# A two-layer transformer with 32 experts: the first four experts' tokens are gathered in two parts

## The chip, the cores and the metric

The kernel runs on one core of one Trainium2 chip, in float32 throughout. The metric is the time of one execution on the device, in microseconds (us). A core has a matrix engine (TensorE, PE in the profile), a vector engine (VectorE, DVE), a scalar engine (ScalarE, ACT), a general engine (GpSimd, POOL) and SyncE (SP), which here does nothing but issue loads. The engines run their own instruction streams side by side and wait for each other through semaphores. 16 DMA engines move data from the chip's memory to the core's.

## The reference: what is computed

256 tokens of width 1024 pass through two hybrid layers (latent attention, a short convolution, a spatial gate, block attention), and then through two layers of attention, each followed by a mixture of experts. Only the mixture matters here:

```python
gates = g_prob * e_prob                      # each token: 1 group of 4, 2 experts of its 8
experts = g_idx * EXPERTS_PER_GROUP + e_local
...
xs = x_pad[row_tok].reshape(n_blocks, MOE_BLOCK, D)      # gather the tokens of each expert
def expert_block(args):
    xb, e = args
    return (jax.nn.silu(xb @ w_gate[e]) * (xb @ w_up[e])) @ w_down[e]
ys = lax.map(expert_block, (xs, block_expert)).reshape(n_rows, D)
out = jnp.zeros((N + 1, D), ys.dtype).at[row_tok].add(ys * row_gate[:, None])[:N]
```

There are 32 experts in each of the two layers. An expert has three matrices, gate and up of 1024 by 512 and down of 512 by 1024, 2 MiB each (2.097 MB); so each expert stage reads 96 matrices, 201 MB.

## The kernel before, in words

An expert stage takes its 32 experts in 8 quads (q = 0 to 7) of four experts (j = 0 to 3). Each expert has room for 32 tokens, so a quad has 128 columns.

- **Gather** (`gather(q)` of `experts`, line 946 on TensorE). A product with a 0/1 selection matrix `SEL` (tokens by 128 columns, written by VectorE in `select`) picks the quad's tokens out of the normalised activations `XH` and turns them at once. 8 chunks of the width, 2 tiles of tokens each, make 16 products with a stationary operand of 128x128 and 128 moving columns; in float32 the profile records each as two instructions, hence x32. Chunks 0 to 3 go to bank 0 and ScalarE moves them to `XG` (with scale and bias), chunks 4 to 7 to bank 1, and VectorE moves them. The records of these products are on line 460, the helper `product`.
- **Gate and up** (line 983). For expert j TensorE multiplies its 32 columns of `XG` with the gate matrix (m = 0), then with the up matrix (m = 1): 8 chunks times 4 column groups, 64 records for each matrix. ScalarE applies silu (line 2067), VectorE multiplies (line 1170), TensorE turns the result (`hidden`, line 456).
- **Down** and **combine**: products with the four down matrices (lines 1017, 1030 and 1046), scaling by VectorE, a product that adds the results to the tokens' rows (line 1076).

TensorE runs, in this order: `gather(0)`; experts 0 to 3 of quad 0; down; `gather(1)`; combine; experts 4 to 7; and so on. The gather of a later quad stands ahead of the down products of the quad before it.

**Loads.** SyncE issues all matrices in the order of their use, into 9 slots of 2 MiB (5 of `ring`, 4 in `AR`). The function `plan` fixes at build time which matrix follows which in a slot. Before a load is issued (line 2586), SyncE waits until the last product that reads the slot's matrix before is done; nothing else holds it back. When an expert stage starts, all nine slots are full: gate and up of experts 0 to 3 and the first down matrix. Three matrices are given back early: expert 0's gate in four quarters, its up in two halves and expert 1's gate in two halves (`PARTS`, semaphore `parts`), so their successors are loaded in eight issues on line 2578, six MiB in all. Expert 1's up is the first to be given back whole.

```python
if c < NC - 1 and c % n == n - 1:
    ins.then_inc(sem("parts"), 1)
```

Of the kernel before, what the change touches and what calls it, by code (L numbers as in the profile page):

```python
# [10 lines left out]
ACT = mybir.ActivationFunctionType  # L11
# [117 lines left out]
def program(nc, A, out):  # L129
    with ExitStack() as ctx:  # L130
# [159 lines left out]
        def filled(*name):  # L290
            b, n = RESULT[name]
            return sem(f"filled{b}"), n

        def drained(*name):
            b, n = RESULT[name]
            return sem(f"drained{b}"), n

        def bank(*name):
            return banks[RESULT[name][0]]
# [141 lines left out]
        def _(eng):  # L441
            pe = Engine(eng, sem("pe"))

            def begin(b, *name):
                if n_results[b]:
                    pe.wait_ge(sem(f"drained{b}"), n_results[b])
                n_results[b] += 1
                RESULT[name] = b, n_results[b]
                return banks[b]

            def end(ins, *name):
                ins.then_inc(filled(*name)[0], 1)
# [5 lines left out]
            def product(o, pairs):  # L458
                for i, (l, r) in enumerate(pairs):
                    ins = eng.matmul(o, l, r, start=i == 0, stop=i == len(pairs) - 1)  # L460
                return ins
# [481 lines left out]
                    end(eng.matmul(o[:, :], ones[0:1, :], dst[0:1, 512 * h:512 * h + 512], start=True, stop=True), "row", k, w, h)  # L943

            def experts(i):
                def gather(q):
                    for b in range(2):
                        o = begin(b, "xg", i, q, b)
                        pe.wait_ge(sem("xn"), 4 * i + 2)
                        pe.wait_ge(sem("sel"), 8 * i + q + 1)  # L950
                        for cc in range(4):
                            ins = product(o[:, 128 * cc:128 * cc + 128],
                                          [(XH[:, t, 128 * (4 * b + cc):128 * (4 * b + cc) + 128],
                                            SEL[q % 2][t].rearrange("p e s -> p (e s)")) for t in range(NT)])
                        end(ins, "xg", i, q, b)

                gather(0)
                for q in range(NQ):
                    u = q % 2

                    def hidden(j):
                        o = begin(4, "aT", i, q, j)
                        pe.wait_ge(*drained("gu", i, q, j))
                        end(turn(o[:, 0:128], AA[j % 2]), "aT", i, q, j)
# [9 lines left out]
                    for j in range(4):  # L974
                        o = begin(2 + j % 2, "gu", i, q, j)
                        for m in range(2):
                            name = "gu", i, 4 * q + j, m
                            w = piece(name, NC, 512)
                            pe.wait_ge(*loaded(*name))
                            for c in range(NC):  # L980
                                pe.wait_ge(*drained("xg", i, q, c // 4))
                                for f in range(4):
                                    ins = eng.matmul(o[32 * f:32 * f + 32, 128 * m:128 * m + 128],  # L983
                                                     XG[u][:, c, 32 * j:32 * j + 32], w[:, c, f::4],
                                                     start=c == 0, stop=c == NC - 1)
                                n = NC // PARTS.get(name, (1, 0))[0]
                                if c < NC - 1 and c % n == n - 1:
                                    ins.then_inc(sem("parts"), 1)
                            if not m:
                                DONE[name] = pe.step(ins)  # L990
                        end(ins, "gu", i, q, j)
                        DONE[name] = filled("gu", i, q, j)
                        if j:
                            hidden(j - 1)
                        if q == NQ - 1 and j == 1:
                            sums = begin_sums()
                    o = begin(4, "gsT", i, q)
# [168 lines left out]
        def _(eng):  # L1166
# [681 lines left out]
                v.tell(eng.tensor_copy(cnt[:, NE:NE + 1], rt(388, 1)), sem("cnt"), i + 1)  # L1848

            def experts(i, chosen):  # L1850
                def gather(q):
                    v.wait_ge(*filled("xg", i, q, 1))
                    if q == 1:
                        v.wait_ge(sem("fin"), i + 1)
                    if q > 1:
                        v.wait_ge(*filled("gu", i, q - 2, 3))
                    for cc in range(4):
                        c = 4 + cc
                        ins = ts(XG[q % 2][:, c, :], bank("xg", i, q, 1)[:, 128 * cc:128 * cc + 128],
                                 COMB[:, 2 * i, 0, c:c + 1], ALU.mult, COMB[:, 2 * i, 1, c:c + 1], ALU.add)  # L1860
                        if cc == 3:
                            free(ins, "xg", i, q, 1)
                        else:
                            v.step(ins)

                gather(0)
                router_end(i, *chosen)
                for q in range(NQ):
                    u = q % 2
# [7 lines left out]
                    for j in range(4):  # L1877
                        w = j % 2
                        bk = bank("gu", i, q, j)
                        v.wait_ge(*filled("gu", i, q, j))  # L1880
                        v.wait_ge(sem("silu"), 32 * i + 4 * q + j + 1)
                        if j > 1:
                            v.wait_ge(*filled("aT", i, q, j - 2))
                        elif q:
                            v.wait_ge(*filled("aT", i, q - 1, j + 2))
                        free(tt(AA[w], bk[:, 128:256], SG[w], ALU.mult), "gu", i, q, j)
                        if j:
                            hidden(j - 1)
                        if j != 2:
                            continue  # L1890
                        if q > 1:
                            v.wait_ge(*filled("cb", i, q - 2, 1, 1))
                        v.wait_ge(sem("sel"), 8 * i + q + 1)
                        for t in range(NT):
                            ins = tt(GS[u][:, t, :].rearrange("p (e s) -> p e s", e=4), SEL[u][t],
                                     bcast(gates[:, t, 4 * q:4 * q + 4], 2, CAP), ALU.mult)
                            if t:
                                v.tell(ins, sem("gs"), 8 * i + q + 1)
                            else:
                                v.step(ins)  # L1900
                        if q + 1 < NQ:
                            select(i, q + 1)
                        if not q:
                            if not i:
                                extract(10)
                            gate_rows(2 + i)
                            if not i:
                                norm_columns(1, 1, 0, "comb1", 1)
# [154 lines left out]
        def _(eng):  # L2063
# [292 lines left out]
                    free(ins, "row", k, w, h)  # L2356

            def experts(i):
                def gather(q):
                    s.wait_ge(*filled("xg", i, q, 0))  # L2360
                    if q == 1:
                        s.wait_ge(sem("fin"), i + 1)
                    if q > 1:
                        s.wait_ge(*filled("gu", i, q - 2, 3))
                    for c in range(4):
                        ins = act(XG[q % 2][:, c, :], bank("xg", i, q, 0)[:, 128 * c:128 * c + 128], ACT.Identity,
                                  bias=COMB[:, 2 * i, 1, c:c + 1], scale=COMB[:, 2 * i, 0, c:c + 1])
                        if c == 3:
                            free(ins, "xg", i, q, 0)
                        else:  # L2370
                            s.step(ins)

                gather(0)
                for q in range(NQ):
                    for j in range(4):
                        n = 32 * i + 4 * q + j
                        s.wait_ge(*filled("gu", i, q, j))
                        if j > 1:
                            s.wait_ge(*drained("gu", i, q, j - 2))
                        elif q:  # L2380
                            s.wait_ge(*drained("gu", i, q - 1, j + 2))
                        s.tell(act(SG[j % 2], bank("gu", i, q, j)[:, 0:128], ACT.Silu), sem("silu"), n + 1)
                    if i and not q:
                        gate_rows(1, "g2", mpart)
                    if q + 1 < NQ:
                        gather(q + 1)
                norm_row(2 * i + 1, 0, LN_OUT[0])
                norm_row(2 * i + 1, 1, LN_OUT[1])
# [392 lines left out]
```

## Time and profile before

| | us |
|---|---|
| median of 3 runs | 1512.19 (1511.61 to 1512.41) |
| the profiled execution | 1512.55 |
| its span | 1510.7 |
| TensorE busy | 1374.3 (91%) |
| VectorE busy | 544.2 (36%) |
| ScalarE busy | 216.3 (14%) |
| DMA, mean over the span | 352 GB/s, 531.20 MB |
| first expert stage, first products | 472.98 |
| second expert stage, first products | 1054.93 |

Times in the trace count from the span's start. In a timeline row the columns are start, length, engine, line, operation, what is written and read, count, and in brackets the idle time before with what ended it. In a row of windows they are the stretch, its length, the busy time (and number) of PE, PEld (loads of the stationary operand), DVE, ACT and POOL, then the clock that TensorE was granted (1.00 is 2.4 GHz, 0.50 is 1.2 GHz), the busy share of the DMA engines and what they moved in GB/s.

A busy TensorE is not the same as a full one: the records of successive products overlap. What holds the kernel must be read stage by stage, from who waits for whom.

### The profile page before, as it was taken

What the parts mean: (1) busy time and instruction counts of PE and PEld (TensorE: products, weight loads), DVE (VectorE), ACT (ScalarE), POOL (GpSimd) and SP (SyncE); (2) the same over time, 40 slices, a digit from 0 to 9 for tenths busy, and PEclk for the clock granted to TensorE, in tenths of its full rate; (3) what the DMA queues carried; (4) which work ended last, traced back from release to release, by engine and by line L of the source; (5) the groups of instructions that cost most, each with busy time, mean ns of one, the idle gap of its engine ahead of it and who ended that gap; (6) DMA issues with size and microseconds to landing.
All of it is one profiled execution on the core that took longest, in us unless ns stands there. A gap on an engine that the chain in (4) does not pass through costs nothing.

```text
span 1510.7 us, 28846 instructions
## 1 busy us (share of the span) xinstructions
PE 1374.3 (91%) x13006; PEld 883.4 (58%) x13006; DVE 544.2 (36%) x1276; ACT 216.3 (14%) x574; POOL 83.5 (6%) x91
## 2 busy tenths in 40 slices
PE   8999999999999999879879799989999798797796
PEld 4886488578887556346345354467575364463443
DVE  3696659675763211111111106555111111111113
ACT  3230123022332000000000001442000000000000
POOL 3100111000003000000000000100200000000000
PEclk9999999999999999899899899999999898998998
DMA  9657955778888999999999999347999999999995
GB/s 347 234 196 258 334 193 197 284 273 301 305 325 324 428 426 426 425 428 426 426 427 426 428 402 343 120 177 307 405 427 426 427 426 427 426 426 429 426 422 211
DMA packets 96534, 531.20 MB, mean 352 GB/s; under 512 B 5248, under 2 KB 7488, under 8 KB 73872
## 3 DMA queue, kind: packets, MB, share of 16 engines
q1 hardware_dynamic: 93248, 519.40, 85.1%
q0 software_dynamic: 3152, 9.86, 1.9%
q8 instruction: 104, 1.70, 0.5%
q14 instruction: 30, 0.25, 0.0%
HBM read 528.19 MB, written 1.05 MB: 350 GB/s over the span
## 4 chain that ended last, share of the span: by engine, by line
PE 62%; DMA 27%; DVE 7%; ACT 1%; SPq 1%; issue 1%; POOL 0%; DVEq 0%; ACTq 0%
PE bk L460 23%; PE bk L983 17%; DMA AR<-in_moe_w_down 17%; DMA ring<-in_moe_w_down 10%; PE bk L1017 7%; PE bk L1076 4%; DVE mpart L1178 3%; PE bk L546 3%; PE bk L456 2%; PE bk L724 1%; ACT AR L2067 1%; PE bk L739 1%; SPq L2586 1%; PE bk L695 1%; PE bk L1030 1%
## 5 line engine op out<-in xcount | busy, mean ns | idle before, releaser
L983 PE MATMUL bk<-ring,AR 128*32 128x128 f32 x4736 | 282.5, 409 | 2.5 <-DMA ring<-in_moe_w_up 2.5
L983 PEld LDWEIGHTS bk<-ring,AR 128*32 128x32 f32 x4736 | 187.8, 127 | 88.9 <-DVE X L1170 6.1
L1170 DVE TENSOR_TENSOR AR<-bk,AR 128x128 f32<-128x128 f32 (+2 forms) x106 | 41.2, 389 | 514.5 <-ACT AR L2067 451.8
L983 PE MATMUL bk<-AR 128*32 128x128 f32 x3456 | 206.5, 409 | 2.4 <-DMA AR<-in_moe_w_up 1.6
L2067 ACT ACTIVATE AR<-bk 128x512 f32<-128x512 f32 (+4 forms) x182 | 75.1, 435 | 914.6 <-PE bk L983 742.3
L983 PEld LDWEIGHTS bk<-AR 128*32 128x32 f32 x3456 | 139.5, 128 | 63.6 <-DMA AR<-in_moe_w_up 3.4
L460 PE MATMUL bk<-AR,ring 128*128 128x256 f32 (+1 forms) x832 | 170.6, 364 | 1.6 <-DVE diag L1170 1.6
L1017 PE MATMUL bk<-ring,AR 128*32 128x512 f32 x384 | 123.5, 734 | 44.2 <-DMA ring<-in_moe_w_down 44.1
L460 PE MATMUL bk<-ring,AR 128*128 128x256 f32 (+1 forms) x608 | 159.2, 419 | 1.4 <-DVE diag L1170 1.1
L460 PEld LDWEIGHTS bk<-AR,ring 128*128 128x128 f32 x832 | 147.4, 190 | 21.4 <-issue 3.5
L1017 PE MATMUL bk<-AR 128*32 128x512 f32 x384 | 114.8, 700 | 27.5 <-DMA AR<-in_moe_w_down 27.5
L460 PEld LDWEIGHTS bk<-ring,AR 128*128 128x128 f32 x608 | 115.2, 192 | 40.4 <-issue 25.9
L1178 DVE SCALAR_TENSOR_TENSOR mpart<-ring,ccol,mpart 128x512 f32<-128x512 f32 x154 | 119.8, 778 | 5.5
L1170 DVE TENSOR_TENSOR AR<-bk,mpart 128x512 f32<-128x512 f32 (+1 forms) x34 | 22.4, 660 | 215.4 <-PE bk L1017 181.5
L456 PE MATMUL bk<-cst,AR 128*128 128x128 f32 (+1 forms) x356 | 63.1, 289 | 19.6 <-DVE AR L1875 11.8
L1017 PEld LDWEIGHTS bk<-ring,AR 128*32 128x32 f32 x384 | 25.7, 130 | 92.1 <-DMA ring<-in_moe_w_down 59.6
L456 PEld LDWEIGHTS bk<-cst,AR 128*128 128x128 f32 (+1 forms) x356 | 40.6, 140 | 54.2 <-issue 26.6
L460 PE MATMUL bk<-AR 128*128 128x128 f32 (+1 forms) x536 | 70.8, 291 | 1.0 <-DVE AR L1170 1.0
L1017 PEld LDWEIGHTS bk<-AR 128*32 128x32 f32 x384 | 25.2, 126 | 75.5 <-DMA AR<-in_moe_w_down 38.4
L460 PEld LDWEIGHTS bk<-AR 128*128 128x128 f32 x536 | 65.2, 197 | 6.8 <-issue 4.7
L1076 PE MATMUL bk<-AR 128*128 128x512 f32 x120 | 56.0, 606 | 1.8 <-DVE AR L1170 1.8
L695 PE MATMUL bk<-ring,AR 128*128 128x512 f32 x128 | 55.5, 594 | 0.0
(178 smaller groups left out, 1001.2 us busy)
## 6 DMA issues: line engine op xcount, KB each, us to landing
ring<-in_moe_w_gate SPq DMA_DIRECT2D x38, 2048.0 KB, 25.8
ring<-in_moe_w_up SPq DMA_DIRECT2D x36, 2048.0 KB, 29.2
AR<-in_moe_w_down SPq DMA_DIRECT2D x30, 2048.0 KB, 33.7
AR<-in_moe_w_up SPq DMA_DIRECT2D x28, 2048.0 KB, 20.8
AR<-in_moe_w_gate SPq DMA_DIRECT2D x26, 2048.0 KB, 36.9
ring<-in_moe_w_down SPq DMA_DIRECT2D x26, 2048.0 KB, 34.1
ring<-in_ada_w SPq DMA_DIRECT2D x24, 2048.0 KB, 11.0
ring<-in_w_in SPq DMA_DIRECT2D x11, 2048.0 KB, 14.9
```

The lines of the kernel that those rows point to most:

```text
L456: return eng.transpose(o, a, ident[0:k, 0:k])
L460: ins = eng.matmul(o, l, r, start=i == 0, stop=i == len(pairs) - 1)
L546: ins = eng.matmul(o[:, 0:n], HT[:, c, t * 128:(t + 1) * 128], w[:, c, :], start=c == 0, stop=c == NC - 1)
L695: ins = eng.matmul(o[:, :], BIG[:, x, OUTS[m] + 128 * t:OUTS[m] + 128 * t + 128], w[:, 2 * m + x, :], start=k + x == 0, stop=k + x == 4)
L724: ins = eng.matmul(o[b][:, a * nk:(a + 1) * nk], g["q"][h][:, t * 128:(t + 1) * 128], g["k"][h][:, 0:nk], start=True, stop=True)
L739: ins = eng.matmul(o[64 * b:64 * b + 64, 128 * x:128 * x + 128], g["v"][2 * x + b][kt], ET[j % 2][:, (2 * b + x) * nkt + kt, :], start=kt ...
L983: ins = eng.matmul(o[32 * f:32 * f + 32, 128 * m:128 * m + 128], XG[u][:, c, 32 * j:32 * j + 32], w[:, c, f::4], start=c == 0, stop=c == N ...
L1017: ins = eng.matmul(o[32 * j:32 * j + 32, :], AT[u][:, j, 32 * f:32 * f + 32], w, start=f == 0, stop=f == 3)
L1076: end(eng.matmul(o[:, :], GST[u][:, 128 * t:128 * t + 128], YS[:, 512 * n:512 * n + 512], start=True, stop=True), "cb", i, q, n, t)
L1170: return eng.tensor_tensor(o, a, b, op)
L1178: return eng.scalar_tensor_tensor(out=o, in0=a, scalar=s, in1=b, op0=op0, op1=op1)
L2067: return eng.activation(o, a, f, **kw)
```

## The change

`gather` gets a name, a first column and a number of columns. `gather(0)` in front of the first quad is replaced by `gather(0, "xg", 0, 64)`, which makes only the 64 columns of experts 0 and 1. The other 64, of experts 2 and 3, are made by `gather(0, "xg2", 64, 64)`, which stands on all three engines behind expert 0 (on TensorE between the up product of expert 0 and the gate product of expert 1). Experts 2 and 3 wait for the second part, experts 0 and 1 for the first. It is done in both expert stages. Nothing changes in the other quads, in `PARTS`, or in SyncE's stream.

```diff
@@ TensorE
-                def gather(q):
+                def gather(q, name="xg", k0=0, n=128):
                     for b in range(2):
-                        o = begin(b, "xg", i, q, b)
+                        o = begin(b, name, i, q, b)
                         pe.wait_ge(sem("xn"), 4 * i + 2)
                         pe.wait_ge(sem("sel"), 8 * i + q + 1)
                         for cc in range(4):
-                            ins = product(o[:, 128 * cc:128 * cc + 128],
+                            ins = product(o[:, 128 * cc:128 * cc + n],
                                           [(XH[:, t, 128 * (4 * b + cc):128 * (4 * b + cc) + 128],
-                                            SEL[q % 2][t].rearrange("p e s -> p (e s)")) for t in range(NT)])
-                        end(ins, "xg", i, q, b)
+                                            SEL[q % 2][t].rearrange("p e s -> p (e s)")[:, k0:k0 + n]) for t in range(NT)])
+                        end(ins, name, i, q, b)
-                gather(0)
+                gather(0, "xg", 0, 64)
...
-                                pe.wait_ge(*drained("xg", i, q, c // 4))
+                                pe.wait_ge(*drained("xg2" if not q and j > 1 else "xg", i, q, c // 4))
...
                         if j:
                             hidden(j - 1)
+                        elif not q:
+                            gather(0, "xg2", 64, 64)
@@ VectorE
-                        ins = ts(XG[q % 2][:, c, :], bank("xg", i, q, 1)[:, 128 * cc:128 * cc + 128],
+                        ins = ts(XG[q % 2][:, c, k0:k0 + n], bank(name, i, q, 1)[:, 128 * cc:128 * cc + n],
                                  COMB[:, 2 * i, 0, c:c + 1], ALU.mult, COMB[:, 2 * i, 1, c:c + 1], ALU.add)
...
-                gather(0)
+                gather(0, "xg", 0, 64)
                 router_end(i, *chosen)
...
                         if j:
                             hidden(j - 1)
+                        elif not q:
+                            gather(0, "xg2", 64, 64)
@@ ScalarE
-                        ins = act(XG[q % 2][:, c, :], bank("xg", i, q, 0)[:, 128 * c:128 * c + 128], ACT.Identity,
+                        ins = act(XG[q % 2][:, c, k0:k0 + n], bank(name, i, q, 0)[:, 128 * c:128 * c + n], ACT.Identity,
                                   bias=COMB[:, 2 * i, 1, c:c + 1], scale=COMB[:, 2 * i, 0, c:c + 1])
...
-                gather(0)
+                gather(0, "xg", 0, 64)
...
                         s.tell(act(SG[j % 2], bank("gu", i, q, j)[:, 0:128], ACT.Silu), sem("silu"), n + 1)
+                        if not q and not j:
+                            gather(0, "xg2", 64, 64)
```

## Rows read from the trace of the kernel before

**Rows 1.** The page: GB/s in 40 equal slices; the chain by engine.

```profile
GB/s 347 234 196 258 334 193 197 284 273 301 305 325 324 428 426 426 425 428 426 426 427 426 428 402 343 120 177 307 405 427 426 427 426 427 426 426 429 426 422 211
PE 62%; DMA 27%; DVE 7%; ACT 1%; SPq 1%; issue 1%; POOL 0%; DVEq 0%; ACTq 0%
```

**Rows 2.** The chain of waits in order of time, first expert stage: start us, us, what.

```profile
467.61 5.44 PE bk L460 x32
578.56 34.77 DMA AR<-in_moe_w_down
613.37 9.45 PE bk L1017 x58
```

**Rows 3.** Timeline, start of the second expert stage: start us, us, engine, line.

```profile
1042.51 1.95 PE L460 MATMUL bk<-wr,AR 128*128 128x36 f32 x16 [0.88 <-ACT AR L2067]
1049.87 0.83 PE L460 MATMUL bk<-AR,ones 128*128 128x32 f32 x6
1051.19 3.81 PE L460 MATMUL bk<-AR 128*128 128x128 f32 x32 [0.49 <-DVE AR L1170]
1053.25 1.50 ACT L2067 ACTIVATE AR<-bk,cst 128x128 f32<-128x128 f32 x4 [3.86 <-PE bk L460]
1054.93 11.27 PE L983 MATMUL bk<-ring,AR 128*32 128x128 f32 x192
1055.11 1.36 DVE L1175 TENSOR_SCALAR AR<-bk,cst 128x128 f32<-128x128 f32 x4 [3.03 <-PE bk L460]
```

**Rows 4.** Line 460, from 468, 1051 and 1042 us: ns min/median/max.

```profile
L460 PEld LDWEIGHTS bk<-AR x15: 198/333/333, 467.9 to 470.8; 128*128 128x128 f32 x15
L460 PEld LDWEIGHTS bk<-AR x32: 187/192/192, 1051.2 to 1054.6; 128*128 128x128 f32 x32
L460 PE MATMUL bk<-wr,AR x16: 272/279/279, 1042.5 to 1044.2; 128*128 128x36 f32 x16
```

**Rows 5.** Windows: engines' busy us, then PE clock, DMA share, GB/s.

```profile
468.00:471.00 3.00, 3.00 (x17) 3.00 (x16) 0.43 (x4) 0.00 (x0) 0.00 (x0) 0.51 1.03 426
```

**Rows 6.** Timeline of the queue SP, first expert stage: start us, us.

```profile
474.14 0.33 SPq L2578 DMA_DIRECT2D ring<-in_moe_w_down  x1
482.51 0.37 SPq L2578 DMA_DIRECT2D ring<-in_moe_w_down  x1
488.07 0.34 SPq L2586 DMA_DIRECT2D AR<-in_moe_w_gate  x1
492.15 0.34 SPq L2586 DMA_DIRECT2D AR<-in_moe_w_up  x1
```

**Rows 7.** Windows of the first stage's DMA from its restart on.

```profile
475.00:476.00 1.00, 1.00 (x24) 0.66 (x20) 0.34 (x3) 0.00 (x0) 0.48 (x1) 1.00 0.82 172
475.00:481.60 6.60, 6.60 (x120) 4.99 (x116) 0.63 (x4) 0.28 (x1) 6.02 (x2) 1.00 0.94 308
475.00:487.00 12.00, 12.00 (x212) 9.62 (x208) 0.63 (x4) 0.28 (x1) 10.81 (x4) 1.00 0.96 346
475.00:492.05 17.05, 17.05 (x293) 12.78 (x289) 1.12 (x6) 0.56 (x2) 10.81 (x4) 1.00 0.99 370
475.00:496.90 21.90, 21.90 (x374) 15.61 (x370) 1.78 (x10) 0.83 (x3) 10.81 (x4) 1.00 1.00 384
```

**Rows 8.** The same in the second expert stage: an issue, and a window.

```profile
1064.43 0.37 SPq L2578 DMA_DIRECT2D ring<-in_moe_w_down  x1
1057.00:1068.00 11.00, 11.00 (x196) 8.28 (x192) 0.58 (x4) 0.28 (x1) 10.46 (x4) 1.00 0.94 340
```

**Rows 9.** Later in the first stage: an issue, and three windows.

```profile
524.39 7.73 SPq L2586 DMA_DIRECT2D AR<-in_moe_w_down  x3
495.86:524.39 28.53, 26.86 (x308) 16.02 (x311) 10.76 (x28) 2.06 (x6) 0.00 (x0) 1.00 1.01 426
524.39:563.75 39.36, 38.11 (x551) 23.10 (x544) 5.33 (x18) 2.62 (x8) 0.00 (x0) 1.00 1.01 427
605.00:613.00 8.00, 1.92 (x2) 0.18 (x2) 0.00 (x0) 0.00 (x0) 0.00 (x0) 0.69 1.02 430
```

More of the change, by code:

```diff
@@ L1850, in experts, with gather @@
             def experts(i, chosen):
-                def gather(q):
-                    v.wait_ge(*filled("xg", i, q, 1))
+                def gather(q, name="xg", k0=0, n=128):
+                    v.wait_ge(*filled(name, i, q, 1))
                     if q == 1:
@@ L1858, in gather @@
                         c = 4 + cc
-                        ins = ts(XG[q % 2][:, c, :], bank("xg", i, q, 1)[:, 128 * cc:128 * cc + 128],
+                        ins = ts(XG[q % 2][:, c, k0:k0 + n], bank(name, i, q, 1)[:, 128 * cc:128 * cc + n],
                                  COMB[:, 2 * i, 0, c:c + 1], ALU.mult, COMB[:, 2 * i, 1, c:c + 1], ALU.add)
                         if cc == 3:
-                            free(ins, "xg", i, q, 1)
+                            free(ins, name, i, q, 1)
                         else:
                             v.step(ins)
-                gather(0)
+                gather(0, "xg", 0, 64)
                 router_end(i, *chosen)
@@ L2358, in experts, with gather @@
             def experts(i):
-                def gather(q):
-                    s.wait_ge(*filled("xg", i, q, 0))
+                def gather(q, name="xg", k0=0, n=128):
+                    s.wait_ge(*filled(name, i, q, 0))
                     if q == 1:
@@ L2365, in gather @@
                     for c in range(4):
-                        ins = act(XG[q % 2][:, c, :], bank("xg", i, q, 0)[:, 128 * c:128 * c + 128], ACT.Identity,
+                        ins = act(XG[q % 2][:, c, k0:k0 + n], bank(name, i, q, 0)[:, 128 * c:128 * c + n], ACT.Identity,
                                   bias=COMB[:, 2 * i, 1, c:c + 1], scale=COMB[:, 2 * i, 0, c:c + 1])
                         if c == 3:
-                            free(ins, "xg", i, q, 0)
+                            free(ins, name, i, q, 0)
                         else:
                             s.step(ins)
-                gather(0)
+                gather(0, "xg", 0, 64)
                 for q in range(NQ):
```

## The prediction, made before the changed kernel ran

> **What bounds the kernel now.** I read first the page's slices: in slices 14 to 23 and 30 to 39, about 490 to 870 us and 1095 to 1470 us, the DMA moves 420 to 430 GB/s with hardly a dip [rows 1]. These are the two expert stages. The page's chain names PE for 62% of the span [rows 1], so the second view is the chain in order of time. In the first expert stage it runs over the gather (467.61 us) and the products of quads 0 and 1, and from 578.56 us on over the landing of a down matrix, 34.77 us, before the next down products can go at 613.37 [rows 2]. Near there, from 605 to 613 us, PE is busy for 1.92 of 8.00 us while the DMA moves 430 GB/s [rows 9]. So from quad 2 on the stage is held by the DMA, and PE waits for it in each quad. In quads 0 and 1 PE runs without such waits, but what it does there matters only through the slots that it gives back: a stage ends when its last matrix has landed, and that is when the DMA started, plus bytes by rate, plus every moment in which the queue was dry.
>
> The third view is therefore SyncE's queue against the DMA's windows. Before the stage the nine slots fill and the DMA runs dry; it restarts with the first quarter of expert 0's gate matrix, given back at 474.14 us [rows 6]. Bytes flow in the window 475 to 476 us, at 172 GB/s with a share of 0.82 [rows 7]. By the share they begin at 475.2, by the bytes at the next windows' pace of some 308 GB/s at 475.4: from issue to bytes 1.0 to 1.3 us. From there on the queue never runs dry before: 4 MiB (4.19 MB) are issued ahead of the issue at 482.51 us (expert 1's gate, first half), and the DMA has moved 346 x 12.0 = 4.15 MB by 487.0, so it is through with them at 487.1. With 6 MiB (6.29 MB) it is through at 492.05 (370 x 17.05 = 6.31), four us after the next matrix was issued at 488.07. With 8 MiB at 496.9 (384 x 21.9 = 8.41) [rows 6, 7].
>
> Two things decide then: whether the first quarter is given back earlier, and whether the queue still holds when expert 1's matrices come later.
>
> **First part: the gather in front.** In the second stage the 32 records of the full gather take 3.81 us; less the last one's length of 0.28 that is 0.114 us from one to the next [rows 3]. The change leaves their number and halves the moving columns, 128 to 64. No product of 64 columns on 128x128 operands stands in these rows, but its neighbours do on both sides: with 36 columns 16 records take 1.95 us, with a record of 0.279, so (1.95 - 0.28) / 15 = 0.111 us apart; with 32 columns 6 take 0.83, so 0.11 apart [rows 3, 4]. Between 32 and 128 columns the spacing hardly moves: each product has its own stationary operand, and its load is what repeats every 0.11 us. 32 x 0.003 = 0.1 us is saved. The bounds are 0 and 0.1 us, and I take 0.1.
>
> In the first stage the gather takes 5.44 us [rows 2], since the granted clock is 0.51 from 468 to 471 us [rows 5], the lower level (1.2 GHz). There the load of a stationary operand takes 333 ns instead of 192 [rows 4], so loads slow down as well, and halving the columns saves no more there either. I take 0.1 us again.
>
> The Trainium skill has a rule that speaks for a saving: "TensorE: Matmul & The Clock Gate", Back-to-back issue gap, gives the isolated gap of two matmuls as N / 2.4 + 2.5 ns for N moving columns, which would halve the gather. The same section says that this undercounts where each matmul has its own LDWEIGHTS, and LDWEIGHTS goes by its section with the stationary operand's columns, 128 here in all cases; the two spacings above agree with that. What the first rule would make of the time is the second rival below.
>
> Moving the columns to `XG` gets shorter too, but is not what the first product waits for. ScalarE is done at 1053.25 + 1.50 = 1054.75; the last record of the gather starts by 1054.73 (1055.00 less 0.28), the first product a spacing or two behind, at 1054.93. Chunk 4 comes half a matrix later, near 1056.8, and VectorE is done at 1055.11 + 1.36 = 1056.47 [rows 3]. So the first quarter is given back 0.1 us earlier, no more.
>
> **Second part: the gather behind expert 0.** It adds 16 products, 32 records, at 0.111 to 0.114 us: 3.6 us on PE, in each stage. Behind it in PE's stream stands everything of experts 1 to 3. ScalarE's four moves (1.50 us at 128 columns) and VectorE's four (1.36) [rows 3] lie beside expert 1's products, some 7.5 us long (11.27 us for 192 records, 128 records for an expert [rows 3]), and only expert 2 needs them: nothing. Banks 0 and 1 have been free since 1056.47, six us earlier. VectorE's router end comes a little sooner, not later. SyncE's stream and GpSimd's are untouched; no instruction and no load is moved past them.
>
> So all that SyncE issues from 482.51 us on is issued 3.6 - 0.1 = 3.5 us later. What that does to the DMA, in the first stage:
> - Expert 1's gate, first half: issued at 486.0. The queue holds until 487.1, new bytes come 1.0 to 1.3 us after the issue, at 487.0 to 487.3: a gap of 0 to 0.2 us. The second half, some two us behind, comes in time.
> - These 2 MiB took 492.05 - 487.1 = 4.95 us and are through at 492.05 to 492.25. Expert 1's up is issued at 488.07 + 3.5 = 491.6, bytes at 492.6 to 492.9 instead of 492.05. All told the DMA is 0.5 to 0.85 us late.
> - The next one is issued at 492.15 + 3.5 = 495.65, bytes by 496.95, and the queue holds until 497.4 or later. PE gives back a matrix every 3.8 us or so, the DMA needs 4.9 for one: from here the backlog grows again.
> - A restart is not at full pace at once (172 GB/s in the window 475 to 476 [rows 7], against 426 later [rows 9]): up to 0.6 us for a full one. For two near-empty moments I add 0.4 us.
>
> Sum: 0.7 + 0.4 = 1.1 us for the DMA, less 0.1 for the earlier start: 1.0 us in the first stage. The second stage has the same pattern: the same half is issued at 1064.43, so 3.5 us later at 1067.9, and by 1068.0 the DMA had moved 340 x 11.0 = 3.74 of 4.19 MB, 1.05 us more of work [rows 8]. 1.0 us again.
>
> Later in the stage the 3.5 us are covered. By 524.39 us SyncE has issued 24 MiB, 25.17 MB (six in eight small issues, nine whole ones), and the DMA has moved 8.41 MB up to 496.9 and 27.5 x 0.426 = 11.7 MB more: a backlog of 5.05 MB, 11.8 us. By 563.75 it has issued eight more, 41.9 MB, and moved 20.1 + 39.36 x 0.427 = 36.9 MB: 11.7 us [rows 7, 9]. PE itself gets its delay back in the 6.1 us that it is idle from 605 to 613 us [rows 9].
>
> The Trainium skill ("DMA: Bandwidth & Descriptors", Specifications) gives a first-byte latency of about 0.6 us for loads issued by SyncE. The trace shows 1.0 to 1.3 us here. By the page the up matrix's bytes would come at 492.2, the gap would close nearly to nothing, and the sum would be 0 to 0.5 us a stage.
>
> For the profiled execution: 1512.55 + 2 x 1.0 = 1514.55 us. It lies 0.36 us above the median of the runs, so for the median 1512.2 + 2.0 = **1514.2 us**. A measurement of this kernel can tell about 0.2%, 3.0 us, from no change; by that the forecast is "the same", on the slow side.
>
> **Rivals.**
> - **A thin queue is slow (slower).** While the first small issues ran, the DMA moved 308 GB/s over 6.6 us [rows 7], against 426 later. I put this down to the small pieces. If instead it is the short queue that costs, the change brings it back: it decides where the backlog is under one matrix, from 484 to 493 us, and the 2 MiB of expert 1's gate at 308 GB/s take 6.8 instead of 4.95 us, 1.9 us more a stage. 1512.2 + 2 x (1.0 + 1.9) = 1518.0 us. For it: the backlog is half of what it was. Against: by 487.0 the pace had risen, (4.15 - 2.03) / 5.4 = 392 GB/s, while the backlog was no greater. Its end, with no cover at all, is 2 x 3.5 us: 1519.2.
> - **Half the columns, half the price (faster).** Then the gather in front is 1.8 us shorter, the second costs only 1.8, expert 1 comes when it did, and each stage's DMA starts 1.8 us earlier (2.0 in the first, at the low clock): 1512.2 - 3.8 = 1508.4 us. Against it stand the 36 and 32 columns.
> - **The clock.** In the first stage it rises during the gather, at about 471 us. With half as many columns streamed it may rise later or, in the second stage, fall. 16 records at 0.21 instead of 0.114 us are 1.5 us, and another such stretch of 3 us at the lower level over the first products 1.5 us more, ahead of the first quarter and so in full: 1512.2 + 2.0 + 3.0 = 1517.2 us. For it: it did fall at 468 us. Against: the sixteen 36-column products kept their length from first to last, 272 to 279 ns [rows 4].
> - **Nothing gets through.** The bytes come faster behind a queue that still moves than after a dry one; the backlog covers all: 1512.2 - 0.2 = 1512.0 us.
>
> **How the numbers follow.** Forecast 0.58, thin queue 0.15, clock 0.09, nothing 0.12, half price 0.06. Faster by over 0.2% is the half price alone: 0.06. Slower by over 0.2% (above 1515.2) is the thin queue, the clock, and a little of the forecast's upper end: 0.27. The same: 0.67. The range takes in "nothing" with something to spare below, and nearly all of the thin queue: 1511.2 to 1518.0.
>
> **What would show it.** In the profile after: the 32 records in front of the first products still take 3.6 to 3.8 us in the second stage, and 32 more stand between experts 0 and 1, with the same spacing; the first quarter is given back at the same time to 0.2 us; the issues from expert 1's gate on are 3.5 us later; the DMA's windows show a dip near 487 and 492 us, and the same bytes 1 us later from then to the stage's end. I am wrong if the gather in front takes under 3 us, if the dips cost over 2 us a stage, or if there are none.

## The result, and the profile after

The changed kernel takes 1520.2 us in the median of 5 runs (1518.82 to 1520.98), against 1512.41 of the kernel before (1511.61 to 1513.92) beside it. The ratio is 1.0051, 95% interval 1.004 to 1.0062: slower by 6 to 9.4 us. The profiled execution took 1518.86 us, with a span of 1517.1 against 1510.7, so it is at the lower end of its runs and has 6.4 us of the difference.

The page's slices and the chain's shares look as before [rows 1]: both expert stages are still held by the DMA.

```profile
GB/s 347 229 194 258 335 193 199 285 265 302 313 325 297 420 426 426 426 427 426 427 427 426 427 402 335 120 183 306 378 428 427 426 426 426 426 426 428 426 423 217
PE 62%; DMA 27%; DVE 7%; SPq 2%; ACT 1%; issue 1%; POOL 0%; DVEq 0%; ACTq 0%
```

The 13th and the 14th slice, where the first stage starts, have lost (324 and 428 before, 297 and 420 now), and so has the 29th, where the second does (405, 378). The chain of waits in order of time (start us, us, what) shows the new step in each stage, the gather between two runs of expert products, and then the same landing as in [rows 2]:

```profile
468.36 6.16 PE bk L460 x32
474.53 7.49 PE bk L983 x124
482.01 3.71 PE bk L460 x32
...
583.95 34.40 DMA AR<-in_moe_w_down
618.39 9.30 PE bk L1019 x58
...
914.92 1.11 PE bk L1058 x8
...
1056.02 3.76 PE bk L460 x32
...
1067.23 3.71 PE bk L460 x32
...
1499.05 1.11 PE bk L1058 x8
```

The chain's last step of each stage that waits for a piece of the last down matrices stood here in the kernel before, in the same view:

```profile
909.96 1.11 PE bk L1056 x8
...
1492.67 1.11 PE bk L1056 x8
```

With SyncE's first issue of each stage on line 2584 (475.64 and 1060.87 us; before 474.14 and 1056.09) the span falls into parts:

| us | before | after | difference |
|---|---|---|---|
| to the first gather | 467.61 | 468.36 | +0.75 |
| first stage, gather to first issue ("front") | 6.53 | 7.28 | +0.75 |
| first stage, first issue to last matrix ("behind") | 435.82 | 439.28 | +3.46 |
| between the stages | 141.23 | 141.10 | -0.13 |
| second stage, front | 4.90 | 4.85 | -0.05 |
| second stage, behind | 436.58 | 438.18 | +1.60 |
| rest | 18.03 | 18.05 | 0.0 |

The first line lies ahead of anything that was changed. The change's own cost is 0.75 in front and 5.06 us behind. How the bytes flow behind a first issue is seen in windows cut from it, 0 to 12 and 12 to 26 us. First the second stage of the kernel before:

```profile
1056.09:1068.09 12.00, 12.00 (x214) 8.96 (x210) 1.46 (x9) 0.28 (x1) 10.55 (x4) 1.00 0.87 316
1068.09:1082.09 14.00, 14.00 (x238) 9.32 (x234) 3.16 (x10) 0.55 (x2) 0.20 (x1) 1.00 1.03 427
```

and of the kernel after, with two single us out of it:

```profile
1060.87:1072.87 12.00, 12.00 (x180) 8.85 (x176) 2.29 (x12) 1.57 (x5) 10.57 (x4) 1.00 0.89 321
1072.87:1086.87 14.00, 14.00 (x242) 9.23 (x234) 0.70 (x4) 0.55 (x2) 0.00 (x0) 1.00 0.97 362
...
1074.00:1075.00 1.00, 1.00 (x24) 0.68 (x18) 0.00 (x0) 0.00 (x0) 0.00 (x0) 1.00 0.88 217
1085.00:1086.00 1.00, 1.00 (x24) 0.43 (x13) 0.00 (x0) 0.00 (x0) 0.00 (x0) 1.00 0.86 229
```

In this stage the first 12 us are alike. Then the DMA moves 362 instead of 427 GB/s for 14 us: 0.91 MB, 2.1 us of work. It is not idle for that long. In the two dips shown its share is 0.88 and 0.86 while it moves about half of its bytes: the engines count as busy and carry little. The first stage, before and then after, is not alike from the start:

```profile
474.14:486.14 12.00, 12.00 (x212) 9.37 (x208) 1.46 (x9) 0.28 (x1) 10.55 (x4) 1.00 0.89 316
486.14:500.14 14.00, 14.00 (x240) 9.12 (x234) 4.25 (x13) 0.56 (x2) 0.27 (x1) 1.00 1.03 429
```

```profile
475.64:487.64 12.00, 12.00 (x180) 8.78 (x176) 2.27 (x12) 1.57 (x5) 10.63 (x4) 0.98 0.86 288
487.64:501.64 14.00, 14.00 (x239) 8.75 (x231) 0.68 (x3) 0.55 (x2) 0.00 (x0) 1.00 1.00 378
```

After 12 us it has moved 0.34 MB less, 0.8 us, nearly all of it lost in the first 8, in which SyncE issued as before: this restart was slow by itself. In the next 14 us it loses 0.71 MB, 1.7 us.

### The profile page after: what moved, and what is told of

Read it like the earlier page. It is cut to its first block, busy times and chain, and to the rows that moved or that the text cites. A ratio compares the mean times of both kernels' runs of the same rounds, so it can differ in the third digit from the quotient of the medians.

```text
span 1517.1 us, 28992 instructions
## 1 busy us (share of the span) xinstructions
PE 1383.1 (91%) x13070; PEld 891.5 (59%) x13070; DVE 545.9 (36%) x1284; ACT 218.5 (14%) x582; POOL 83.2 (5%) x91
## 4 chain that ended last, share of the span: by engine, by line
PE 62%; DMA 27%; DVE 7%; SPq 2%; ACT 1%; issue 1%; POOL 0%; DVEq 0%; ACTq 0%
PE bk L460 23%; DMA AR<-in_moe_w_down 17%; PE bk L983 16%; DMA ring<-in_moe_w_down 9%; PE bk L1019 7%; PE bk L1078 4%; DVE mpart L1180 3%; PE bk L546 3%; PE bk L456 2%; SPq L2592 2%; PE bk L724 1%; ACT AR L2071 1%; PE bk L739 1%; PE bk L695 1%; PE bk L1032 1%; PE bk L558 1%
## 5 line engine op out<-in xcount | busy, mean ns | idle before, releaser
L1019 PE MATMUL bk<-AR 128*32 128x512 f32 x384 | 117.9, 711 | 27.2 <-DMA AR<-in_moe_w_down 27.2
L460 PE MATMUL bk<-AR 128*128 128x128 f32 (+3 forms) x600 | 79.0, 291 | 1.0 <-DVE AR L1172 1.0
L460 PEld LDWEIGHTS bk<-AR 128*128 128x128 f32 x600 | 73.2, 198 | 7.6 <-issue 5.5
```

The lines of the kernel that those rows point to most:

```text
L1019: ins = eng.matmul(o[32 * j:32 * j + 32, :], AT[u][:, j, 32 * f:32 * f + 32], w, start=f == 0, stop=f == 3)
```

## The experiments

For each, "front" and "behind" are read from its profile as in the table above. The ratio is of its runs to those of the kernel before beside it, with its 95% interval. A "front" or "behind" stands for one execution only, and the profiled one need not lie at its median.

**e1.** Full gather in front; the delay behind expert 0 alone.

```diff
+                def extra(k):
+                    for b in range(2):
+                        pe.wait_ge(*drained("xg", i, 0, b))
+                        for cc in range(k):
+                            product(banks[b][:, 128 * cc:128 * cc + 64], ... SEL[0] ... [:, 0:64])
...
                         if j:
                             hidden(j - 1)
+                        elif not q:
+                            extra(4)
```

> The kernel before with its full gather in front, plus 16 unused products of 64 columns (32 records, 3.65 us) on TensorE behind expert 0 in each expert stage; ScalarE and VectorE as before. This is the changed kernel without the narrow gather in front. Theory S (the loss is the later issue of everything behind expert 0, into a queue that is nearly empty and therefore slow): the DMA is 2.1 to 2.5 us behind in each stage as in the changed kernel, +4.5 to +6.5 us in all. Theory C (the narrow columns in front hold TensorE's clock down, and that is most of the loss): +2 us or less, and the gather in front takes 5.4 us in the first stage, not 6.2. Theory G (my forecast: two short gaps, 1.1 us a stage): +2.2 us.

Measured: 1518.0 us, ratio 1.0036 (1.0023 to 1.0049). Behind: 439.67 and 438.46, +3.85 and +1.88. Theory S: the delay alone, with ScalarE, VectorE and the front as before, makes the whole loss behind. The profiled execution took 1521.03 us, 3.0 above the median, and has 3.1 us more than the kernel before between the stages, where nothing was changed (144.32 against 141.23). More than half of that is one run of 16 records from 1047.59 us on, at a granted clock of 0.50: 3.60 us instead of 1.95. Its fronts took 4.90 us in both stages: in this execution the clock didn't fall before the first gather. So C can't be judged by it, and what its median lacks to the changed kernel's may be in front, which is not shown.

**e2.** The same with half of the products, `extra(2)`.

> As e1, with 8 unused products (1.8 us) instead of 16 behind expert 0. Theory G (gaps only): the backlog of 4.6 us before expert 1's gate matrix is issued covers a delay of 1.8 us wholly, so 0.0 us. Theory S (a short queue moves less even when it isn't empty): about a third to a half of e1's loss, +1.5 to +3 us. Were every us of delay lost: +3.6 us.

Measured: 1514.5 us, 1.0009 (1.000 to 1.0018). Behind: 436.71 and 436.55, +0.89 and -0.03. In the windows 12 to 26 us after the first issue, first stage and then second:

```profile
487.55:501.55 14.00, 14.00 (x238) 8.80 (x234) 2.34 (x10) 0.56 (x2) 0.16 (x1) 1.00 1.01 394
...
1070.34:1084.34 14.00, 14.00 (x238) 8.99 (x234) 2.42 (x9) 0.56 (x2) 0.12 (x1) 1.00 1.02 424
```

By the stages' ends the second has theory G's zero, the first about a fourth of e1's. The bytes speak for S in both: summed from the first issue to 428 us behind it, the DMA is 0.8 and 0.7 us behind the kernel before, a third of e1's 2.4 and 2.0. The loss doesn't grow with the delay in proportion: by the ends 1.8 us cost 0.9 in two stages and 3.6 us cost 5.7, by the bytes 1.5 and 4.4. So more than half of the first 1.8 us is covered, and of the next 1.8 us little.

**e3.** `gather(0)`, then `extra(4)` at once, both in front of the first product.

> The kernel before with the same 16 unused products in front of the first product instead of behind expert 0. The DMA's restart comes 3.65 us later in each stage and nothing thins the queue afterwards. Theory: a delay in front is lost in full, +7.3 us, and the DMA's bytes against its first issue run as before. If the changed kernel's +7.8 us is about this, then standing behind expert 0 shelters nothing.

Measured: 1519.4 us, 1.0045 (1.0032 to 1.0058). The first issues, the last products and the windows 12 to 26 us behind:

```profile
478.09 4.97 SPq L2587 DMA_DIRECT2D ring<-in_moe_w_down  x5
...
1064.17 6.84 SPq L2587 DMA_DIRECT2D ring<-in_moe_w_down  x6
```

```profile
913.89 1.11 PE bk L1065 x8
...
1500.74 1.11 PE bk L1065 x8
```

```profile
490.09:504.09 14.00, 14.00 (x238) 9.16 (x234) 4.33 (x14) 0.56 (x2) 0.00 (x0) 1.00 1.03 425
...
1076.17:1090.17 14.00, 14.00 (x238) 9.00 (x234) 3.16 (x10) 0.56 (x2) 0.00 (x0) 1.00 1.03 424
```

Behind: 913.89 - 478.09 = 435.80, and 1500.74 - 1064.17 = 436.57. The kernel before has 435.82 and 436.58. So in these two executions a stage's length from the first issue on agrees to 0.02 us, as the supply behind it keeps its rhythm, and what is late in front is lost in full (3.53 and 3.59 us, 7.1 of the 7.3 forecast). This is the yardstick for all the others, though e7 below, with nearly the same supply, lies 0.4 and 0.6 us off it. It also says that the changed kernel's second gather, put behind expert 0, saved in the second stage 2 us of its 3.7, and in the first next to nothing, if the stages' ends are taken (by the bytes moved, see below, some 1.6 us in both).

**e4.** The changed kernel with the second part behind expert 1 (`if not q and j == 1`, on all three engines).

> The changed kernel with its second part behind expert 1 instead of expert 0. Expert 1's matrices are given back as early as before; from expert 2's gate on all is 3.6 us later. Theory G: the queue holds by 1 us at the next issue, loss 0 to 0.5 us a stage, +0 to +1 us. Theory S: the queue is near its end once instead of twice, 0.5 to 1.5 us a stage, +1.5 to +3.5 us. Theory C (clock in front): the same as the changed kernel less nothing, as the front is the same: the part of the loss that is the clock's stays, some +1.5 us in either case.

Measured: 1516.2 us, 1.0022 (1.0013 to 1.0032). Behind: 436.91 and 437.18, +1.09 and +0.60. Windows 12 to 26: 416 and 417 GB/s. The same 3.7 us one expert later cost 1.7 instead of 5.1 us, when a matrix more has been given back. Its front in the first stage took 7.82 us, 1.29 more than before (the changed kernel's 0.75).

**e5.** The changed kernel with 16 unused narrow products more in front, 64 records in all.

> The changed kernel with 16 more unused products of 64 columns in front, behind the narrow gather: 64 records in front, 32 behind expert 0. Against e3 (32 records of 128 columns and 32 of 64 in front, 8.97 us in the first stage, of which 1.6 us is the lower clock) only the width of the first 32 differs. Theory C (a stream of 64 columns doesn't raise the clock once it is low): in the first stage the clock stays low through the whole front, 11 to 13 us instead of 8.97. Theory W (width has no part in it, the clock rises when it did): 9.0 us. In both, the delay behind expert 0 costs the DMA the 2 to 2.5 us a stage that it cost in the changed kernel, so about +13 us against the kernel before, and 2 to 4 us more in theory C.

Measured: 1529.8 us, 1.0105 (1.009 to 1.012). Behind: 438.47 and 438.80, +2.65 and +2.22. The timeline's two fronts, and windows of the first:

```profile
467.92 13.45 PE L460 MATMUL bk<-AR 128*128 128x64 f32 x64 [0.49 <-DVE AR L1181]
...
1062.05 7.33 PE L460 MATMUL bk<-AR 128*128 128x64 f32 x64 [0.49 <-DVE AR L1181]
```

```profile
469.00:485.00 16.00, 16.00 (x126) 14.96 (x130) 1.88 (x10) 2.57 (x5) 8.18 (x4) 0.50 0.26 94
486.00:487.00 1.00, 1.00 (x24) 0.62 (x20) 0.00 (x0) 0.00 (x0) 1.00 (x1) 1.00 1.02 303
```

Against e3's 8.97 us, of which half are 128 columns wide, 13.45: a little above theory C's range. The clock fell in the front's first us and stayed at 0.50 for the rest of it, and for four us of expert 0's products behind it. In the second stage it stayed high, and the same 64 records took 7.33 us. The first stages of the other executions in which the clock fell show the same difference. In those with a gather of 128 columns it was low for 3.4 us and rose within the gather (the kernel before, e2, e3, e7). In those with the narrow gather it was low for 6.8 us (changed kernel, e6), 10.2 (e4) and 17.1 (e5), and rose only behind it, in expert 0's products. What the fall costs the front also hangs on when it comes: e6, where it came two us into the gather, has a front of 6.46 us, and the kernel before 6.53. How TensorE ran in the changed kernel's front, line 460 between 469.8 and 474 us:

```profile
L460 PE MATMUL bk<-AR x22: 421/421/421, 469.4 to 473.9; 128*128 128x64 f32 x22
L460 PEld LDWEIGHTS bk<-AR x21: 333/333/333, 469.5 to 473.8; 128*128 128x128 f32 x21
```

All 22 are at the lower level, where the kernel before had some 16 of its 32 there. The Trainium skill ("TensorE: Matmul & The Clock Gate", What's actually happening) has the clock set by how busy TensorE has been of late; by the records TensorE was without a pause at either width, so no run here shows why the narrow gather's clock stayed low for longer. The whole came out as expected, 16 us above the kernel before.

**e6.** The changed kernel, with expert 1's up and expert 2's gate given back in halves too.

```diff
-        PARTS = {("gu", i, j, m): (n, 5 * i + k) for i in range(DEPTH) for j, m, n, k in ((0, 0, 4, 1), (0, 1, 2, 4), (1, 0, 2, 5))}
+        PARTS = {("gu", i, j, m): (n, 7 * i + k) for i in range(DEPTH)
+                 for j, m, n, k in ((0, 0, 4, 1), (0, 1, 2, 4), (1, 0, 2, 5), (1, 1, 2, 6), (2, 0, 2, 7))}
```

> The changed kernel with two more matrices given back in halves, expert 1's up and expert 2's gate, so that 1 MiB of each is issued 1.9 us earlier just where the queue is short. Theory S (a short queue is what loses the time): the DMA is less behind at 26 us from its first issue, 0.3 to 0.8 us gained a stage, so 0.6 to 1.6 us faster than the changed kernel. If the delay as such were what counts: the same time as the changed kernel.

Measured: 1519.4 us, 1.0034 (1.0022 to 1.0045). Behind: 438.62 and 438.21, so 0.66 better than the changed kernel in the first stage and the same in the second. At 26 us from the first issue it has moved 0.08 and 0.12 MB more than the changed kernel, 0.2 and 0.3 us. That is at or below the low end of S and doesn't decide. By chance it shows something else, its second front:

```profile
1056.06 5.40 PE L461 MATMUL bk<-AR 128*128 128x64 f32 x32 [0.49 <-DVE AR L1173]
```

5.40 against 3.76 us of the changed kernel: the clock fell here at 1058 us, in the midst of the gather. So the lower clock can meet the narrow gather in the second stage as well.

**e7.** The kernel before with the same halves.

> The kernel before with the same two matrices given back in halves. Its queue is about four us deep at those issues; theory S: 0 to 0.3 us a stage, the same time. Smaller issues could also cost: 1 MiB pieces instead of 2 MiB, up to +0.5 us a stage.

Measured: 1513.4 us, 0.9997 (0.9988 to 1.0005). Behind: 436.19 and 436.03, +0.37 and -0.55. No difference that can be measured, as forecast: where loads are issued four us ahead, a finer supply gave nothing.

**e8.** The kernel before with the first gather split by width.

```diff
-                gather(0)
+                gather_pair(0)
+                gather_pair(1)
...
+                                if not (q or j or m) and c == 4:
+                                    gather_pair(2)
+                                    gather_pair(3)
```

`gather_pair(p)` makes chunks 2p and 2p + 1 in a bank of its own; ScalarE moves chunks 0 to 3 and VectorE chunks 4 to 7, each pair when it is there.

> The kernel before with the first gather split by width instead of by expert: chunks 0 to 3 (all 128 columns, 16 records) in front, chunks 4 to 7 between chunk 3 and chunk 4 of expert 0's gate products. The same 32 records in all, so nothing behind expert 0 is later. The first quarter is given back 1.6 to 1.9 us earlier, the third at the old time. e3 showed that a delay of the first issue is paid in full; if an advance is earned in full: -3.4 us in all. If the queue then runs dry between the second and third quarter, as the 1 MiB given back early lasts only 2.5 us: -0.5 to -1 us a stage, -1 to -2 us in all (my forecast).

Measured: 1512.8 us, 0.9996 (0.9985 to 1.0006). SyncE's first issues and the last products:

```profile
472.54 12.67 SPq L2612 DMA_DIRECT2D ring<-in_moe_w_down  x8
...
1054.73 12.67 SPq L2612 DMA_DIRECT2D ring<-in_moe_w_down  x8
```

```profile
910.46 1.03 PE L1070 MATMUL bk<-AR 128*32 128x512 f32 x8
...
1492.46 1.07 PE L1070 MATMUL bk<-AR 128*32 128x512 f32 x8 [0.60 <-DMA AR<-in_moe_w_down]
```

The second front is 1054.73 - 1051.46 = 3.27 us instead of 4.90, so 1.63 were gained; behind it is 437.73 instead of 436.58, so 1.15 were given back. 0.5 us net, the least that was forecast. In the first stage, where the clock did not fall in front, 472.54 - 469.23 = 3.31 us, 1.59 less than 4.90, and 2.10 were given back: 0.5 us lost. So the advance was not earned; over both stages of the profiled execution nothing is left of the 1 to 2 us forecast, though the interval of the ratio doesn't exclude them. The dry spell between the second and the third quarter fits this and was not tested by itself. None of the kernels beats the one before.

## Why the prediction was wrong

By its steps:

- **What bounds the stages** held: e3's stages behind the first issue agree with those of before to 0.02 us.
- **The gather in front at the high clock**: right. Halving the columns saved 0.05 us (4.90 to 4.85), 0.1 was forecast. Half columns were not half price.
- **The gather in front at the low clock**: wrong, 0.75 us lost where 0.1 was to be saved (in e4's execution 1.29, in e6's 0.07 saved). The step "loads slow down as well, and halving the columns saves no more there either" was right about the price at either level, and silent on how long the lower one lasts. That stood among the rivals at 0.09. e5 shows its mechanism in the front. Its second half, a further slow stretch over the expert products, came and cost nothing: they took 7.56 us for 128 records in the changed kernel though their first 1.6 us had the lower clock, and 7.53 in e5 with it for four us.
- **How late all behind expert 0 is issued**: right. In the second stage expert 1's gate came 1072.96 - 1060.87 = 12.09 us behind the first issue instead of 8.34, its up 17.64 instead of 13.90: 3.75 us, and 3.6 was forecast.
- **The later backlog covers it, PE gets its delay back from quad 2 on**: right; from 30 us behind the first issue on the DMA is back at 426 GB/s or more.
- **What the DMA loses to that delay**: wrong, and this is the step that failed. "For two near-empty moments I add 0.4 us" and the gaps of 0.7 made 1.1 us a stage; it was 3.46 and 1.60 by the stages' ends, and 2.1 and 2.0 by the bytes moved. I counted only the time in which the queue is empty. The windows show the loss as dips in which the DMA is busy and slow, and one of them, 1085 to 1086 us, has more than 2 MB issued and unmoved: 8.39 MB given back up to 1078.51 and 2.10 more at 1082.58, less some 8.4 moved. There the queue's end was one matrix away, issued about 2.4 us before its turn. By the bytes moved expert 1's gate and its up were each issued 1.2 us before their turn. In the kernel before each of these was issued some four us or more before its turn [rows 6, 7], and from 12 to 26 us no window of 2 us is under 410 GB/s. That is the rival of the thin queue, at 0.15; its price, 2.9 us a stage, was near the mean of the two, 2.5. Whether the dips come from the short queue as such, or are what is left of a restart when the next load comes just in time, is not settled: e6, which was to tell, gained too little.

That rival's 2.9 us a stage and the front's 0.7 make 6.5 us. The profiled executions differ by 6.4, of which 0.75 lie ahead of the stages: 5.7 us for these two causes.

One reading behind the gaps was coarse. "From issue to bytes 1.0 to 1.3 us" came from windows of one us. In windows of 0.2 us the first bytes come 0.8 us after the issue, at a quarter to a third of the later pace, and it takes about two us from the issue to some 350 GB/s:

```profile
474.74:474.94 0.20, 0.20 (x12) 0.14 (x4) 0.18 (x2) 0.00 (x0) 0.00 (x0) 1.00 0.00 0
474.94:475.14 0.20, 0.20 (x12) 0.12 (x5) 0.20 (x3) 0.00 (x0) 0.00 (x0) 1.00 0.87 102
475.34:475.54 0.20, 0.20 (x12) 0.12 (x8) 0.04 (x1) 0.00 (x0) 0.03 (x1) 1.00 0.52 102
475.94:476.14 0.20, 0.20 (x8) 0.15 (x4) 0.00 (x0) 0.00 (x0) 0.20 (x1) 1.00 1.02 348
```

By their ends the first stage loses about two us more than the second at the same delay (changed kernel 3.46 and 1.60, e1 3.85 and 1.88, e2 0.89 and 0; e5 has 2.65 and 2.22). By the bytes it doesn't. Summed over windows of 20 to 40 us, up to 428 us behind the first issue, the DMA of the changed kernel is 0.9 MB behind the kernel before in either stage, 2.1 and 2.0 us (e1 2.4 and 2.0, e5 2.0 and 2.2; good to some 0.2 us). The other 1.3 us of the first stage, and the 0.4 that the second gets back, arise in the last eight to eleven us before the stage's end.

What stays open: why the ends differ so. And the median's further 1.4 us over the profiled execution: longer stretches at the lower clock, as in e4's first and e6's second front or in e1 between the stages, would do it, but this is not shown.

## What to carry to other kernels

Where a stage is bound by loads, cut the timeline at the stage's first issue: a delay in front of it is paid one for one, and one behind it is free only while every load is issued well ahead of its turn, not merely before the queue is empty: here four us ahead cost nothing, and 1.2 to 2.4 us ahead left dips. Splitting a product by its moving columns saved nothing here, as each product loads its own 128 columns of stationary operand: the same 32 records took 3.76 us instead of 3.81, and came twice. Splitting it by the stationary side (e8) keeps the number of loads. And half-wide products can cost more than their time at the upper clock: read the granted clock over them and behind them.

## What the runs showed of the hardware that was not expected

- A stream of float32 products of 64 columns on 128x128 operands, without a pause, stayed at a granted clock of 0.50 for some 12 us (e5). In the four executions where the clock fell at the start of the gather of 128 columns, it was back at 1.00 after 3.4 us.
- The products of line 983 (stationary 128x32, four column groups side by side) took 7.53 us for 128 records while the clock was 0.50 for their first four us (e5), and 7.55 at 1.00 throughout (e1): the lower clock cost them nothing, while it took the gather's records from 0.114 to 0.21 us apart.
- With a share of 0.86 to 0.88 the DMA moved 217 to 229 GB/s (changed kernel, the two dips), where at 1.00 it moves 426. The share alone doesn't tell that a queue is well fed; the GB/s do.
